# Stick-breaking attention by an exponential of z minus the inclusive suffix sum, with the mask put in by a matmul

## What is computed

```
z = einsum('bqhd,bkhd->bhqk', qblk, k) * scale + bias
mask = key_idx[None, :] < qpos[:, None]
log_1mb = where(mask, log_sigmoid(-z), 0.0)
acc = cumsum(log_1mb, axis=3, reverse=True) - log_1mb
wts = where(mask, exp(log_sigmoid(z) + acc), 0.0)
o = einsum('bhqk,bkhd->bqhd', wts, v)
```

## Time and profile before

| | |
|---|---|
| median of 3 runs | 2354.62 us (2353.75 to 2356.7) |
| the profiled execution | 2357.5 us, span 2355.8 us |
| TensorE busy | 2245.6 us |
| VectorE busy | 1122.0 us |
| ScalarE busy | 784.9 us |
| GpSimd busy | 115.3 us |
| heads of `stick`, first score to last copy | 1774.20 to 1876.37 us |
| samples after them, to the output projection | to 1901.8 us |

### The profile page before, as it was taken

One profiled execution on the slowest core, in us unless ns is written; L12 is line 12 of the kernel. 1 busy time (PEld: TensorE's weight loads), 2 busy tenths in 40 slices (PEclk: granted clock), 3 DMA queues, 4 the chain that ended last, 5 costly groups with the idle time before them and its releaser, 6 DMA issues.

```text
span 2355.8 us, 43642 instructions
## 1 busy us (share of the span) xinstructions
PE 2245.6 (95%) x17746; PEld 2157.8 (92%) x17746; DVE 1122.0 (48%) x1673; ACT 784.9 (33%) x1064; POOL 115.3 (5%) x186
## 2 busy tenths in 40 slices
PE   7999999998889899999999999999998799999997
PEld 7999999997778799999999999999994379999996
DVE  5444433764346554444334444433667744444332
ACT  4222222352233443222223222223456533222222
POOL 2000000100112200000000000000003200000000
PEclk9999999998889999999999999999998999999998
DMA  4333333422200123333333333333323133333331
GB/s 123 96 90 89 89 90 91 117 81 55 60 9 1 45 86 98 90 89 91 89 95 92 89 89 91 93 90 89 90 81 109 45 90 90 94 93 89 92 89 52
DMA packets 352976, 195.70 MB, mean 83 GB/s; under 512 B 9903, under 2 KB 347979, under 8 KB 352873
## 3 DMA queue, kind: packets, MB, share of 16 engines
q1 hardware_dynamic: 344640, 172.36, 25.4%
q0 software_dynamic: 6064, 19.86, 2.8%
q10 hardware_dynamic: 2176, 2.15, 0.3%
HBM read 186.43 MB, written 8.04 MB: 83 GB/s over the span
## 4 chain that ended last, share of the span: by engine, by line
PE 66%; DVE 4%; ACT 3%; issue 1%; DMA 0%; POOL 0%; POOLq 0%; ACTq 0%; DVEq 0%
PE PS L1753 57%; PE PS L1861 5%; PE PS L2199 1%; PE PS L2167 0%; PE PS L2188 0%; PE PS L2040 0%; DVE skX L1602 0%; DVE Dm L1435 0%; DVE skX L1617 0%; PE PS L2151 0%; ACT skX L1020 0%; ACT skL L1029 0%; ACT skL L1028 0%; ACT skL L1026 0%; ACT skY L1023 0%
## 5 line engine op out<-in xcount | busy, mean ns | idle before, releaser
L1753 PE MATMUL PS<-hh,whi 128*128 128x260 f32 x3600 | 733.1, 285 | 7.8 <-DVE hl L1681 6.5
L1753 PE MATMUL PS<-hh,wlo 128*128 128x260 f32 x3600 | 728.3, 284 | 0.0
L1753 PE MATMUL PS<-hl,whi 128*128 128x260 f32 x3600 | 727.5, 284 | 0.0
L1121 DVE TENSOR_TENSOR wlo<-stage,whi 128x1024 fp32r<-128x1024 f32 x337 | 413.3, 1226 | 459.3 <-ACT whi L692 448.2
L1753 PEld LDWEIGHTS PS<-hh,whi 128*128 128x128 f32 x3600 | 560.0, 190 | 11.3 <-DVE hl L1681 4.8
L1753 PEld LDWEIGHTS PS<-hh,wlo 128*128 128x128 f32 x3600 | 558.0, 189 | 0.0
L1753 PEld LDWEIGHTS PS<-hl,whi 128*128 128x128 f32 x3600 | 557.1, 189 | 0.0
L692 ACT ACTIVATE whi<-stage 128x1024 fp32r<-128x1024 f32 x337 | 352.8, 1048 | 254.1 <-PE PS L1753 245.4
L1753 PE MATMUL PS<-act_h,whi 128*128 128x260 f32 x1408 | 283.9, 283 | 0.0
L1753 PE MATMUL PS<-act_h,wlo 128*128 128x260 f32 x1408 | 283.1, 282 | 0.0
L1753 PE MATMUL PS<-act_l,whi 128*128 128x260 f32 x1408 | 282.5, 282 | 0.0
(11 more groups left out here) (383 smaller groups left out, 1792.0 us busy)
## 6 DMA issues: line engine op xcount, KB each, us to landing
stage<-in_ffn_w_gate SPq DMA_DIRECT2D x88, 512.0 KB, 3.8
stage<-in_ffn_w_up SPq DMA_DIRECT2D x88, 512.0 KB, 3.8
stage<-in_ffn_w_down SPq DMA_DIRECT2D x64, 512.0 KB, 4.1
stage<-in_w_in_e SPq DMA_DIRECT2D x28, 512.0 KB, 3.7
stage<-in_ffn_w_down SPq DMA_DIRECT2D x32, 384.0 KB, 3.4
stage<-in_w_in_o SPq DMA_DIRECT2D x20, 512.0 KB, 3.9
stage<-in_w_out_e SPq DMA_DIRECT2D x8, 512.0 KB, 4.1
stage<-in_w_out_o SPq DMA_DIRECT2D x8, 512.0 KB, 4.1
```

Source lines behind the costliest of these rows:

```text
L1121: dve.tensor_tensor(wlo[:, slot, :], stage[:, s % STAGE_SLOTS, :], whi[:, slot, :].bitcast(F32), ALU.subtract).then_inc(lo_ready, 1)
L1753: mm = pe.matmul(psum[:, half, :], w, x(k)[:, half * HALF:(half + 1) * HALF], start=first and w is hi and x is rhs_hi, stop=last and w is lo)
```

## The change

With L = softplus(z) the weight is sigmoid(z) times exp of minus the sum of L over later keys, and since log sigmoid(z) = z - L this is exp(z - S), where S is the sum over this key and all later ones. The changed kernel computes it so: one read of the scores into `skZ` (three buffers in a ring), the minimum of z and 40 on VectorE, exp, ln(1 + it), and the maximum of z and that as the softplus. An inclusive triangle `upto` takes the place of `after` for the prompt. `skR` is gone: ones-matmuls run over each later block by itself, six a head instead of three. The mask is put into the scores before they are read: a matmul of the identity with the tile `hide` (0 or -2^60), one for each diagonal piece, in the one-pass type; both softplus and weight then come out as 0. So neither VectorE nor GpSimd masks. The queries of the samples are stored to a DRAM tensor `q_rows` and loaded back one row at a time, spread over 128 partitions, by GpSimd's queue, two buffers in `tmp`. A sample's product and reduction take both pages at once. TensorE makes the scores two heads ahead.

```diff
+                def scores(h):
+                    act.wait_ge(sk_z, h + 1)
+                    if h >= 3:
+                        act.wait_ge(sk_o, h - 2)
+                    act.activation(skZ[:, h % 3, :], banks(0, 3)[:, 0:SCORES], ACT.Identity, bias=sbb[:, 0, h:h + 1])\
+                       .then_inc(sk_read, 1)
+                scores(0)
                 for h in range(HC + 2):
                     if h < HC:
-                        act.activation(skX[:, h % 2, :], z, ACT.Relu, bias=sbb[:, 0, h:h + 1])
-                        act.activation(skY[:, h % 3, :], z, ACT.Relu, scale=-1.0, bias=sbb[:, 1, h:h + 1])
-                        act.activation(skL[:], z, ACT.Abs, bias=sbb[:, 0, h:h + 1]).then_inc(sk_read, 1)
-                        link(act.activation(skL[:], skL[:], ACT.Exp, scale=-1.0))
+                        act.wait_ge(sk_cut, h + 1)
+                        link(act.activation(skL[:], skL[:], ACT.Exp))
                         act.activation(skL[:], skL[:], ACT.Ln, bias=1.0).then_inc(sk_ln, 1)
+                    if h + 1 < HC:
+                        scores(h + 1)
                     if 1 <= h <= HC:
+                        n = h - 1
+                        act.wait_ge(sk_sub, n + 1)
+                        act.activation(skZ[:, n % 3, :], skZ[:, n % 3, :], ACT.Exp).then_inc(sk_w, 1)
...
+                def cut(h):
+                    dve.wait_ge(sk_read, h + 1)
+                    dve.tensor_scalar(skL[:], skZ[:, h % 3, :], STICK_CLAMP, None, ALU.min).then_inc(sk_cut, 1)
+                cut(0)
                 for h in range(HC):
                     dve.wait_ge(sk_ln, h + 1)
+                    dve.tensor_tensor(skX[:, h % 2, :], skZ[:, h % 3, :], skL[:], ALU.max).then_inc(sk_sp, 1)
+                    if h + 1 < HC:
+                        cut(h + 1)
                     sample_scores(h)
+                    dve.wait_ge(sk_acc, h + 1)
+                    dve.tensor_tensor(skZ[:, h % 3, :], skZ[:, h % 3, :], banks(3, 3)[:, 0:SCORES], ALU.subtract)\
+                       .then_inc(sk_sub, 1)
...
             def sample_scores(b):
-                dve.wait_ge(sm_q, b + 1)
+                dve.wait_ge(q_loaded[b % 2], 16 * (b // 2 + 1))
                 dve.wait_ge(page_loaded[b % 4], 16 * PAGES * (b // 4 + 1))
+                q = qrow[:, b % 2:b % 2 + 1, :].to_broadcast([P, PAGES, WC])
+                link(dve.tensor_tensor(kq, pages[:, b % 4], q, ALU.mult))
+                dve.tensor_reduce(smS[:, 0, :, b, :], kq.rearrange("p a (h d) -> p a h d", h=HC), AX.X, ALU.add)\
...
+                def score(h):
+                    if h:
+                        pe.wait_ge(sk_read, h)
+                    for n, (at, w) in enumerate(SCORE):
+                        z = banks(0, 3)[:, at:at + w]
+                        pe.matmul(z, prO[r, OK + h // 2, n * P:(n + 1) * P], prO[r, OQ + h // 2, n * P:TP],
+                                  start=True, stop=False)
+                        mm = pe.matmul(z[:, 0:P], ident_r[:], hide_r[:], start=False, stop=True)
+                    mm.then_inc(sk_z, 1)
+                score(0)
+                score(1)
+                for h in range(HC + 1):
+                    if h + 2 < HC:
+                        score(h + 2)
...
+                            mm = pe.matmul(acc, upto[:], skX[:, h % 2, at:at + w], start=True, stop=n == NB - 1)
+                            for c in range(n + 1, NB):
+                                at_c, w_c = SCORE[c]
+                                mm = pe.matmul(acc[:, w - w_c:], ones[:], skX[:, h % 2, at_c:at_c + w_c], start=False,
+                                               stop=c == NB - 1)
...
+                pool.wait_ge(v_rows, NB + 1)
+                pool.dma_start(q_rows, rowS[:, 0, :]).then_inc(q_saved, 16)
...
+                pool.wait_ge(q_saved, 16)
+                load_q(0)
+                load_q(1)
                 for n in range(HC):
                     pool.wait_ge(sm_kq, n + 1)
                     load_pages(n + 4)
-                    pool.wait_ge(sk_w, n + 1)
-                    for at, _ in SCORE:
-                        block_w = skY[:, n % 3, at:at + P]
-                        last = pool.tensor_tensor(block_w, block_w, before[:], ALU.mult)
-                    last.then_inc(sk_mask, 1)
+                    if n + 2 < TS:
+                        load_q(n + 2)
```

More of the change, by code:

```diff
@@ L36 @@
 CLAMP = 80.0
+FAR = 2.0 ** 60
+STICK_CLAMP = 40.0
 LOOKAHEAD = 3
@@ L265, in build_step @@
         after = sb("after", [P, P], F32, st)
-        before = sb("before", [P, P], F32, st)
+        upto = sb("upto", [P, P], F32, st)
+        hide = sb("hide", [P, P], F32, st)
+        hide_r = sb("hide_r", [P, P], F32R, st)
+        ident_r = sb("ident_r", [P, P], F32R, st)
         sbb = sb("sbb", [P, 2, HC], F32, st)
@@ L374, in build_step @@
         k_rows = sem("k_rows")
-        sk_z, sk_read, sk_ln, sk_added, sk_sp, sk_acc, sk_add, sk_w, sk_mask, sk_o, sk_oc = (
-            sem("sk_" + n) for n in "z read ln added sp acc add w mask o oc".split())
+        sk_z, sk_read, sk_cut, sk_ln, sk_sp, sk_acc, sk_sub, sk_w, sk_o, sk_oc = (
+            sem("sk_" + n) for n in "z read cut ln sp acc sub w o oc".split())
         page_loaded = [sem(f"page_loaded{n}") for n in range(4)]
-        sm_q, sm_kq, sm_ln, sm_w, sm_pv, sm_oc = (sem("sm_" + n) for n in "q kq ln w pv oc".split())
+        q_saved, q_loaded = sem("q_saved"), [sem(f"q_loaded{n}") for n in range(2)]
+        sm_kq, sm_ln, sm_w, sm_pv, sm_oc = (sem("sm_" + n) for n in "kq ln w pv oc".split())
         sm_step = sem("sm_step")
@@ L1598, in stick @@
             def stick():
-                def mask(buf, a):
-                    for at, _ in SCORE:
-                        last = dve.tensor_tensor(buf[:, a, at:at + P], buf[:, a, at:at + P], before[:], ALU.mult)
-                    return last
-                dve.wait_ge(o_consts, CONSTS + 5)
-                def add_later(n):
-                    dve.wait_ge(sk_acc, n + 1)
-                    dve.tensor_tensor(skY[:, n % 3, :], skY[:, n % 3, :], banks(3, 3)[:, 0:SCORES], ALU.add)\
-                       .then_inc(sk_add, 1)
+                def cut(h):
+                    dve.wait_ge(sk_read, h + 1)
+                    if h:
+                        dve.wait_ge(sk_sp, h)
+                    dve.tensor_scalar(skL[:], skZ[:, h % 3, :], STICK_CLAMP, None, ALU.min).then_inc(sk_cut, 1)
@@ L1612, in stick @@
+                cut(0)
                 for h in range(HC):
-                    a = h % 2
-                    if h:
-                        add_later(h - 1)
                     dve.wait_ge(sk_ln, h + 1)
-                    link(dve.tensor_tensor(skX[:, a, :], skX[:, a, :], skL[:], ALU.add))
-                    link(mask(skX, a))
-                    x1, x2, x3 = (skX[:, a, at:at + w] for at, w in SCORE[1:])
-                    w1 = TP - P
-                    dve.tensor_copy(skR[:, w1:w1 + P], x2[:, 0:P])
@@ L1633, in sample_scores @@
                 dve.wait_ge(page_loaded[b % 4], 16 * PAGES * (b // 4 + 1))
-                for p in range(PAGES):
-                    link(dve.tensor_tensor(kq[:], pages[:, b % 4, p, :], banks(7, 1), ALU.mult))
-                    last = dve.tensor_reduce(smS[:, 0, p, b, :], kq[:].rearrange("p (h d) -> p h d", h=HC), AX.X, ALU.add)
-                    if p < PAGES - 1:
-                        link(last)
-                last.then_inc(sm_kq, 1)
-                dve.wait_ge(sm_kq, b + 1)
+                if b:
+                    dve.wait_ge(sm_kq, b)
@@ L2131, in stick @@
                 pe.wait_ge(k_rows, NB + 2)
-                for h in range(HC + 2):
+                pe.wait_ge(o_consts, CONSTS + 9)
+                def score(h):
+                    r = slice(h % 2 * HDC, (h % 2 + 1) * HDC)
+                    if h:
+                        pe.wait_ge(sk_read, h)
[5 more added lines that the diff above has]
+                    mm.then_inc(sk_z, 1)
@@ L2150, in stick @@
                             acc = banks(3, 3)[:, at:at + w]
-                            mm = pe.matmul(acc, after[:], skX[:, a, at:at + w], start=True, stop=n == NB - 1)
-                            if n < NB - 1:
-                                mm = pe.matmul(acc[:, P:], ones[:], later[n], start=False, stop=True)
-                        mm.then_inc(sk_acc, 1)
-                    if h < HC:
-                        if h:
-                            pe.wait_ge(sm_kq, h)
-                        mm1(banks(7, 1), row_of(h)(TS), rowS[:, 0, :]).then_inc(sm_q, 1)
```

81 lines of the change are left out of this document (32 added, 49 removed).

## The result

The changed kernel takes 2377.11 us (median of 4 runs, 2376.9 to 2378.69) where the kernel before takes 2354.61: a ratio of 1.0091, with a 95% interval of 1.0078 to 1.0104. It is 22.5 us slower. The forecast was 2349.2 us, in a range of 2343.5 to 2355.5.

The account below looks back on a forecast made before the run. TensorE was taken to bound the changed steady heads; these lose 3.3 us, first and last heads win 8.7, so 5.4 off the median 2354.6 gives 2349.2 us, range 2343.5 to 2355.5.

Parts of the forecast that it names:

- The sign: Whole change: the last head's copy ends 5.4 us earlier, giving 2349.2 us; chance of faster by over 0.2%: 0.57.
- rival 3: TensorE's clock falls to 1.2 GHz inside steady heads, 8.5 us more each; four give 2383 us; chance 0.07.
- the new wait: Ahead of the scores of head h+3, TensorE stands while ScalarE reads those of head h+2: 1.5 us.
- The steady turn: Each of four steady heads: 9.8 us of TensorE work plus 1.5 of waiting, 11.3 us against 10.50 before.
- The masks: Four one-pass mask matmuls in each head's scores: 0.12 us each, bounds 0.05 and 0.39; scores become 2.9 us.
- rival 2: Mask matmuls cost as f32 ones, 0.39 us each: 4.9 off the gain, 2354.1 us; chance 0.12.
- The fill: First heads, from 1774.2 us: head 1's suffix sum late and 2.3 us slower at low clock; product 0 ends 1806.3.
- A: Theory of the follow-ups: TensorE's clock falls because of the new wait, time in which it stands idle.
- B: Theory of the follow-ups: the clock falls from the stretch between suffix sums with TensorE on half its array or idle.
- The query row: First sample's query row, issued at 1786.7 us, lands between 1790.0 and 1792.2, taken as 1791.5, delaying head 1's suffix sum.
- rival 1: First query row comes in time, or the clock stays up: 9.2 us off, 2345.4 us; chance 0.20.
- Drain and the rest: Behind the steady heads: from 1851.5 us to the last copy's end at 1871.0; the samples' part stays 25.4.

Follow-up runs that it names:

- Experiment 1: Changed kernel with the scores of head h+2 made behind the output product, so TensorE's wait goes: 2349.57 us, ratio 0.9982 to the kernel before.
- experiment 2: Changed kernel without the four mask matmuls of each head, the wait of 1.5 us kept: 2351.3 us in one execution.
- experiment 4: Kernel with scores moved behind the output product, plus six filler matmuls between product and scores: 2365.22 us over 64 rows, 2358.19 over 128.
- the last kernel: Kernel with masks in a row, scores behind the output product and VectorE block sums, plus query-row store and two loads earlier in GpSimd's queue: 2341.06 us.
- 3: Changed kernel with the wait filled by six matmuls of 128 columns: 2362.52 us over 128 rows, 2369.32 over 64.
- the second half of 5: Changed kernel, wait kept, with the four masks of a head made first in a row: 2353.17 us in one execution.

## Why the prediction was wrong, step by step

**The sign.** The step that failed is rival 3 and its price of a chance: "Gaps are shorter than now, so it is unlikely". It was wrong twice. The 1.76 us of the earlier trace rows is ScalarE's idle time; TensorE's own gaps in a steady head are 0.54, 0.50 and 0.48 (the two rows below the table), so that the new wait of 1.48 is nearly three times the longest of them. And the step asked only whether TensorE works. The runs show that what it works on counts too: from the output product to the next sum it is on half its array or idle, 5.2 us in the kernel before and 7.7 in the changed one, the short masks included: the wait adds 1.5 and the masks 1.5, and the 0.5 of handover that stood there goes. Experiment 1 shows that without the wait the clock stays, experiment 2 that without the masks it stays in three turns of four, experiment 4 that the fall needs no idle time at all. The rival's mechanism, "one gap of 1.5", was thus a part of the cause. Its price was too high: a head with a fall cost 4.8 us more (17.0 for 12.2), not 8.5, since the clock comes back within the sum and the first part of the scores runs before it falls.

**The steady turn**, 11.3 forecast, 16.6 measured over four. Of the 5.3 that it is off, the masks are 0.9 (fillers of 128 rows, which fill the wait and keep the clock, leave a turn of 12.2) and the clock 4.4. Sum 4.48 for 4.55, product 2.37, wait 1.48 for 1.5: these terms hold, and the turns of 11.32 with the masks in a row show their sum.

**The masks**, 0.12 each by the chain row, measured 0.36 (1.45 for four). That row is of a stream of one kind; the masks stand between f32 matmuls. The upper bound, 0.39, and rival 2 had it. In a row they cost 0.15.

**The fill**, to the end of product 0: 32.1 us from the stage's start forecast (1806.3 - 1774.2), 38.6 measured. The sum of head 0 was to start 12.1 us into the stage and started at 21.0. The scores of heads 1 and 2 took 7.1 and 6.9 us, not 2.9. In the changed kernel's timeline:

```profile
1777.87 2.07 PE L2146 MATMUL PS<-prO 64*128 64x512 f32 x2 [1.48 <-ACT skZ L1033]
1779.87 0.47 PE L2148 MATMUL PS<-hide_r,ident_r 128*128 128x128 f32 x1
...
1786.42 2.07 PE L2146 MATMUL PS<-prO 64*128 64x512 f32 x2 [1.42 <-ACT skZ L1033]
...
1793.36 2.02 PE L2162 MATMUL PS<-skX,upto 128*128 128x512 f32 x2
```

They are at the low level from their first instruction. The forecast priced them at full clock although has PEclk 0.50 from 1780 to 1786: this could be read before. The low clock in sum 1, which the forecast did price (2.3), came in sum 0 instead; sum 1 had no gap and ran at full clock. Why every variant, and the kernel before, is cold in the fill was not tested apart; the stage opens with waits and half-array work, which fits A and B alike.

**The query row** was issued 1785.02 and used at 1790.64, 5.6 us later: the bound from the small stores (5.5) and not the 3.3 of the pages.

```profile
1785.02 1.13 POOL L616 DMA_DIRECT2D tmp<-q_rows  x2
...
1790.64 1.22 DVE L1642 TENSOR_TENSOR tmp<-pages,tmp 128x1024 f32<-128x1024 f32 x1 [3.41 <-DMA tmp<-q_rows]
```

The Trainium skill, DMA: Bandwidth & Descriptors, on the anatomy of one DMA, gives 2.6 us by estimate; behind the stores it was twice that. VectorE waited 3.41 us, but TensorE was at the scores of head 2 till 1793.36, so the row was not on the path; rival 1 could not have mattered. With the masks in a row and no wait it was on the path as the prediction said, until the last kernel brought it earlier.

**Drain and the rest.** From the end of the fourth turn to that of the last copy: forecast 19.5 (1851.5 to 1871.0), measured 19.4. The samples' part 26.0 for 25.4. VectorE's minimum 0.83 for 0.82, its maximum and subtraction 1.49, its product 1.22.

**The sum.** Forecast 96.8 us for the stage, measured 124.4: 27.6 off, of which the fill is 6.5, the four turns 21.1 (masks 3.6, clock 17.5), the drain nothing. The fall in the four turns is not the only step that failed: without its 17.5 us the stage would still be 106.9 by these numbers, 4.7 longer than before and not 5.4 shorter. The longer fill (6.5) was enough by itself to eat the 5.4, and the masks in the turns (3.6) took more than half of it. Experiment 1 is faster than the kernel before by about the gain that was forecast (98.2 us for 102.2), but this is luck as far as the sum goes: it lacks the wait, 6.0 us in the forecast, and pays more for masks and fill.

**What stays open.** Half of the array is 64 rows in the scores and the fillers, and 64 columns in the product; only rows were varied. Each of the kernels behind experiments 2, 3, 4 and the second half of 5 was executed once. The chip's rule is not inferred: the table sets eight kernels side by side, and six of them, with the same instructions in each turn, fall in some turns only.

## What to carry to other kernels

Look for TensorE not only at its gaps but at the whole stretch between runs of full-array work: gaps, matmuls of 64 rows or 64 columns, and short matmuls of other kinds together. A wait of 1.5 us made one turn of four fall by itself and four masks of 0.36 none, but together they made all four fall, at 4.8 us a head, so an edit there is priced with its neighbours and not alone. Move a wait out of such a stretch, put matmuls of one kind in a row, and read the granted clock of every stretch before using a duration from another.

## What the runs showed of the hardware

- TensorE's granted clock fell from 2.4 to 1.2 GHz in stretches in which it was busy for 44.00 of 44.00 us (0.92 and 0.84 in the mean), when fillers over 64 rows were in them. Of the sums behind such fillers seven of nine began slow; behind fillers over 128 rows, of the same number and columns, two of nine.
- A fall costs far more than what sets it off: 1.5 us of wait taken away in each of four turns shortened the four by 23.8 us.
- A one-pass matmul of 128 columns costs 0.15 us in a row of four and 0.36 between f32 matmuls.
- A load of 256 KB issued behind some 2 MB of stores took 5.6 us to its use, in a queue where the median for the eight of these loads is 3.9.
